# First block of a hybrid decoder layer: one input piece between the compression weight halves, two units in halves, scores inside a unit, the scan in parts

## The chip, the cores and the metric

The kernel runs on one core of one Trainium2 chip. The metric is the device time of one execution in microseconds. Three runs of the kernel before took 2506.0, 2507.16 and 2510.76 us; the median is 2507.16 us.

## The reference

A trunk of two equal layers over 256 tokens of width 1024, all in float32. The first block of each layer normalises x, multiplies it by one wide input projection and hands the columns to three branches: a native sparse attention (compressed, selected and windowed keys), a gated linear recurrence (RG-LRU) and a Mamba-2 mixer. The branches are gated, multiplied by branch weights and added to x. The second block (PEER) retrieves single-neuron experts by product keys. What the change touches is all in the first block:

```python
# 15 compressed blocks of 32 tokens, stride 16, for keys and for values
blk = t[:, cmp_idx] + pe[None, None, :, None, :]
return jax.nn.gelu(blk @ w1) @ w2
...
s_c = jnp.einsum('bqghd,bcgd->bghqc', qb, k_cmp) * SCALE      # compressed scores
s_s, s_w = q . k over selected and windowed keys, softmax each
...
b = mult * (i * xc)                                            # RG-LRU
_, h = lax.associative_scan(linear_recurrence_combine, (a, b), axis=1)
```

## The kernel before, in words

The weights come as a stream of *pieces* of 1 MB (128 x 2048 floats), 66 a layer, numbered u. SyncE issues `load(u)` (L315) in order of u into a ring of 4 slots; piece u waits until the work on piece u-4 has been multiplied (`s_proj`). Nearly every piece is split for the exact float32 product: ScalarE writes the rounded high part (`split_hi`, L350, into a ring of 3), VectorE the low part (`split_lo`, L358), and TensorE makes three passes, hi by hi, lo by hi and hi by lo (`three_passes`, L367 to L369). Such a product of one piece with all 256 tokens is a *unit*: 48 matmuls, in two halves of 24 (`feature_half`), one for each 128 output rows. ScalarE takes the result out of PSUM (`take`, L948) and mostly splits the piece three further on in the same step (`next_hi`, `filler`). Each engine runs its list in the order that the program writes; only semaphores join them.

Pieces 8 to 11 are the recurrence's input (LX to LX+3). Pieces 12 to 15 are the compression's first weight matrix, two for keys and two for values (`UNSPLIT`): they aren't split; 64 matmuls (L668) multiply them with shifted blocks that VectorE makes (L1370) from keys and values which TensorE turned (L631, `kv_turned`) and ScalarE took (L1005 to L1010). Pieces 16 to 21 (XBC to XBC+5) are the Mamba input, 22 on the gates.

TensorE's order around the compression is: LX+2, `kv_turned`, LX+3, four weight pieces in two halves of two (L668), two turns of q (L643), XBC, turn of the compressed hidden rows (L679), two turns of q, XBC+1, second compression product (L688, L692), XBC+2, turn (L698), XBC+3, compressed scores of the first tile of 128 tokens (L711), XBC+4. VectorE meanwhile rotates q by position (L1311 to L1321), makes the recurrence's convolution in two halves of four steps (L1378, L1380), takes the turned q (L1396), normalises the compressed keys (L1418 to L1429), and splits XBC to XBC+5 in between.

The attention then runs over 16 pairs n (two tiles of 8). Of each n: TensorE makes scores (L724), VectorE adds mask and takes the maximum (`row_max`, L1466, L1470), ScalarE the exponentials (L1042), VectorE `coefficients` (L1476, L1477), GpSimd scales (L1186), TensorE turns (L740), ScalarE and VectorE take (L1050, L1487), TensorE attends (L763, L767). Between these stands one unit of gates for each n (`FILL[n]`). At n = 8, where the tile changes, come the second compressed scores and two units, `BETWEEN[0]` and `BETWEEN[1]`, each followed by the scores of one pair. VectorE at that place also makes the second half of the recurrence: one product (L1512) and four scans (L1516), with the coefficients of pair 8 between the second and third scan, and it splits `FILL[9]` after them and after `row_max(9)`.

Of the kernel before, what the change touches and what calls it, by code (L numbers as in the profile page):

```python
# [66 lines left out]
UNSPLIT = range(2 * W1K, 2 * XBC0)  # L67
# [119 lines left out]
def trunk(nc, x_in, pos_tok, pos_row, const, wstream, small, rows, mix_row, ffn_row, subkeys, xstream, out):  # L187
    V, A, PE, PO = nc.vector, nc.scalar, nc.tensor, nc.gpsimd
    with ExitStack() as ctx:
# [93 lines left out]
        def layer_programs(layer):  # L283
# [17 lines left out]
            def nth(u):  # L301

                return u if u < UNSPLIT.start else u - len(UNSPLIT)

            def piece(n):

                return n if n < UNSPLIT.start else n + len(UNSPLIT)
# [98 lines left out]
            with mix:  # L406
# [54 lines left out]
                with mid:  # L461
# [65 lines left out]
                    def place(u):  # L527
                        if u < UNSPLIT.start:
                            return u
                        if u < XBC + 5:  # L530
                            return u - 4
# [50 lines left out]
                    def mixer_tensor(pe):  # L582
# [44 lines left out]

                        def kv_turned(t):
# [17 lines left out]
                        for u in range(FIRST, LX + 3):  # L646
# [7 lines left out]
                        for t in range(NT):  # L654
                            kv_turned(t)
                        unit(LX + 3)


                        for half in range(2):
                            w1 = []  # L660
                            for j in range(2):
                                u = UNSPLIT.start + 2 * half + j
# [3 lines left out]
                            for r in range(8):  # L666
                                for j in range(2):
# [132 lines left out]
                        for n in range(1, len(units) + 1):  # L800
# [115 lines left out]
                    def mixer_scalar(act):  # L916
# [37 lines left out]
                        def filler(u):  # L954

                            if u < LG:
                                dst = xbcT[:, 2 * (u - XBC):2 * (u - XBC) + 2, PAD:]
# [33 lines left out]
                        for n in range(3):  # L991
# [8 lines left out]
                        for t in range(NT):  # L1000
                            act.wait_ge(s_kvt, past(s_kvt) + t + 1)
                            for j, c in enumerate((0, 3)):
                                for g in range(G):
# [4 lines left out]
                                    else:  # L1008
# [8 lines left out]
                        act.wait_ge(s_proj, past(s_proj) + UNSPLIT.stop)  # L1017
# [3 lines left out]
                        filler(XBC)  # L1021
# [7 lines left out]
                        filler(XBC + 1)  # L1029
# [1415 lines left out]
```

## Time and profile before

| what | value |
|---|---|
| profiled execution, its own time | 2510.31 us |
| its span | 2508.4 us |
| TensorE matmul busy | 2450.2 us, 98% |
| VectorE, ScalarE, GpSimd busy | 69%, 55%, 32% |
| mean granted TensorE clock | 0.993 |
| chain of work that ended last, TensorE's share | 88% |

The span runs from the first to the last instruction on record; 1.9 us of the execution lie around it. Times in the rows are from the span's start. The first layer's first block takes roughly the first 400 us; the second layer's lies some 1247 us later. A granted clock of 1.00 is the full 2.4 GHz level, 0.50 the 1.2 GHz level.

### The profile page before, as it was taken

To read this page: it belongs to the slowest core of one execution; us is meant where nothing else is said; L and a number is where in the kernel's file an instruction comes from. 1 tells how busy PE (TensorE), PEld (TensorE's weight loads), DVE (VectorE), ACT (ScalarE), POOL (GpSimd) and SP (SyncE) were. 2 spreads that over 40 slices of the span, in tenths; PEclk is the share of its full clock that TensorE was granted. 3 is DMA by queue.
4 is the path that set the end of the run, shared out by engine and by line. 5 is a ranking of instruction groups with operands and counts; after the bars stand their busy time and mean duration, and the time that the engine had idled before them with its cause. 6 is when DMAs were issued, how large, how long until landed. Compare 5 with 4: busy or idle time off the path is not lost.

```text
span 2508.4 us, 45247 instructions
## 1 busy us (share of the span) xinstructions
PE 2450.2 (98%) x18518; PEld 2269.1 (90%) x18518; DVE 1729.8 (69%) x2726; ACT 1388.0 (55%) x2190; POOL 796.9 (32%) x436
## 2 busy tenths in 40 slices
PE   8999999999999999999999999999999999999999
PEld 8898899999999988888798989999999999888887
DVE  6878777499577755555678786764986778555555
ACT  5487564444566654445554965644445666544443
POOL 0011200188898830000000112002888988200000
PEclk9999999999999999999999999999999999999999
DMA  6533335355444455566555333453554444556655
GB/s 253 189 131 114 111 135 193 120 184 184 165 147 150 146 174 194 194 208 236 182 185 185 120 118 117 137 184 133 184 184 163 144 151 146 181 193 193 193 193 168
DMA packets 95963, 419.35 MB, mean 167 GB/s; under 512 B 10768, under 2 KB 11152, under 8 KB 78864
## 3 DMA queue, kind: packets, MB, share of 16 engines
q1 hardware_dynamic: 95760, 416.47, 48.6%
q8 instruction: 149, 2.44, 0.4%
q14 instruction: 54, 0.44, 0.0%
HBM read 415.38 MB, written 1.05 MB: 166 GB/s over the span
## 4 chain that ended last, share of the span: by engine, by line
PE 88%; DVE 6%; DMA 2%; ACT 2%; POOL 1%; issue 0%; SPq 0%; DVEq 0%; ACTq 0%
PE bank L2041 26%; PE bank L367 18%; PE bank L368 17%; PE bank L369 17%; PE bank L2022 3%; DMA xr<-in_xstream 1%; PE bank L763 1%; PE bank L740 1%; PE bank L724 1%; DVE ring_lo L358 1%; POOL xr_lo L1738 1%; DVE choice L2224 1%; PE bank L1880 1%; PE bank L780 1%; PE bank L859 1%; PE bank L872 1%
## 5 line engine op out<-in xcount | busy, mean ns | idle before, releaser
L1733 ACT ACTIVATE xr_hi<-xr 128x1024 fp32r<-128x1024 f32 x512 | 542.3, 1060 | 689.9 <-DMA xr<-in_xstream 686.1
L1738 POOL TENSOR_TENSOR xr_lo<-xr,xr_hi 128x1024 fp32r<-128x1024 f32 x256 | 619.8, 2425 | 409.7 <-ACT xr_hi L1733 408.6
L367 PE MATMUL bank<-featH,xr_hi 128*128 128x256 f32 x2048 | 586.6, 286 | 7.7 <-POOL xr_lo L1738 7.7
L368 PE MATMUL bank<-featL,xr_hi 128*128 128x256 f32 x2048 | 575.2, 281 | 0.0
L369 PE MATMUL bank<-featH,xr_lo 128*128 128x256 f32 x2048 | 574.8, 281 | 0.0
L1738 DVE TENSOR_TENSOR xr_lo<-xr,xr_hi 128x1024 fp32r<-128x1024 f32 x256 | 313.7, 1225 | 303.9 <-ACT xr_hi L1733 303.7
L367 PEld LDWEIGHTS bank<-featH,xr_hi 128*128 128x128 f32 x2048 | 386.0, 188 | 9.1 <-POOL xr_lo L1738 4.8
L368 PEld LDWEIGHTS bank<-featL,xr_hi 128*128 128x128 f32 x2048 | 386.4, 189 | 0.0
L369 PEld LDWEIGHTS bank<-featH,xr_lo 128*128 128x128 f32 x2048 | 385.8, 188 | 0.0
L367 PE MATMUL bank<-featH,ring_hi 128*128 128x256 f32 x1232 | 357.1, 290 | 14.9 <-DVE ring_lo L358 13.7
L368 PE MATMUL bank<-featL,ring_hi 128*128 128x256 f32 x1232 | 351.3, 285 | 0.0
L369 PE MATMUL bank<-featH,ring_lo 128*128 128x256 f32 x1232 | 350.8, 285 | 0.0
L1186 POOL TENSOR_TENSOR tok_z<-tok_z,rst 128x512 f32<-128x512 f32 (+1 forms) x32 | 51.6, 1611 | 864.1 <-DVE rst L1477 864.1
L2041 PE MATMUL bank<-xr_hi,p_hi 128*128 128x512 f32 x1024 | 316.4, 390 | 2.7 <-DVE acts_lo L2272 1.5
L2041 PE MATMUL bank<-xr_lo,p_hi 128*128 128x512 f32 x1024 | 315.3, 389 | 0.0
L2041 PE MATMUL bank<-xr_hi,acts_lo 128*128 128x512 f32 x1024 | 315.3, 389 | 0.0
L358 DVE TENSOR_TENSOR ring_lo<-ring,ring_hi 128x2048 fp32r<-128x2048 f32 x120 | 273.9, 2286 | 59.8 <-ACT ring_hi L350 58.1
L350 ACT ACTIVATE ring_hi<-ring 128x2048 fp32r<-128x2048 f32 x120 | 229.1, 1909 | 98.6 <-PE bank L369 76.5
L367 PEld LDWEIGHTS bank<-featH,ring_hi 128*128 128x128 f32 x1232 | 237.8, 193 | 23.2 <-issue 19.0
L368 PEld LDWEIGHTS bank<-featL,ring_hi 128*128 128x128 f32 x1232 | 237.8, 193 | 0.1
L369 PEld LDWEIGHTS bank<-featH,ring_lo 128*128 128x128 f32 x1232 | 237.6, 193 | 0.0
L2041 PEld LDWEIGHTS bank<-xr_hi,p_hi 128*128 128x128 f32 x1024 | 191.3, 188 | 45.7 <-DVE acts_lo L2272 3.9
(352 smaller groups left out, 4106.9 us busy)
## 6 DMA issues: line engine op xcount, KB each, us to landing
xr<-in_xstream SPq DMA_DIRECT2D x512, 512.0 KB, 3.3
ring<-in_wstream SPq DMA_DIRECT2D x128, 1024.0 KB, 4.9
smw<-in_small SPq DMA_DIRECT2D x4, 617.0 KB, 9.9
first<-in_wstream SPq DMA_DIRECT2D x4, 512.0 KB, 6.9
first<-in_wstream SPq DMA_DIRECT2D x2, 1024.0 KB, 8.3
subk<-in_subkeys SPq DMA_DIRECT2D x2, 1024.0 KB, 7.4
x<-in_x SPq DMA_DIRECT2D x2, 512.0 KB, 5.8
big<-in_mix_row SPq DMA_DIRECT2D x2, 512.0 KB, 4.8
```

What stands on the lines that cost most here:

```text
L350: A.activation(hi, w, ACT.Copy).then_inc(s_hi, 1)
L358: V.tensor_tensor(lo, w, hi.bitcast(F32), ALU.subtract).then_inc(s_lo, 1)
L367: PE.matmul(o, s_hi_lo[0], m_hi_lo[0], start=first, stop=False)
L368: PE.matmul(o, s_hi_lo[0], m_hi_lo[1], start=False, stop=False)
L369: return PE.matmul(o, s_hi_lo[1], m_hi_lo[0], start=False, stop=last)
L724: mm = PE.matmul(bank[2 + g][:, b * nk:(b + 1) * nk], qT[g * DH:(g + 1) * DH, i, t * P:(t + 1) * P], kT[g * DH:(g + 1) * DH, b, 0:nk], sta ...
L740: tr = PE.transpose(bank[4 + k][:, j * P:(j + 1) * P], sc[:, n % 2, j, k * P:(k + 1) * P], ident)
L1186: PO.tensor_tensor(sc[:, n % 2, :, 0:nk], sc[:, n % 2, :, 0:nk], over(rst[:, n % 2, 2, :], nk), ALU.mult).then_inc(s_scaled, 1)
L1733: A.activation(xr_hi[:, m % XR], xr[:, m % XR], ACT.Copy).then_inc(s_xhi, 1)
L1738: (PO if m < NKEY else V).tensor_tensor(xr_lo[:, m % XR], xr[:, m % XR], xr_hi[:, m % XR].bitcast(F32), ALU.subtract).then_inc(s_xlo_pool ...
L2022: mm = PE.matmul(bank[g % GBANKS][:, j * P:(j + 1) * P], hots(g)[:, j, 0, :], hots(g)[:, j, third, :], start=third == 1, stop=third == 3)
L2041: mm = PE.matmul(bank[2 * t + h][:], p, w[:, m % XR, h * 512:(h + 1) * 512], start=first_one and i == 0, stop=last and i == NKEY - 1)
```

## The change

The stream is laid out anew: XBC (now `FIRST_XBC`) becomes piece 14 and stands between the two weight halves, which are pieces 12, 13 and 15, 16. TensorE turns keys and values before LX+2 instead of after it; after LX+3 it multiplies the first weight half, then the unit of piece 14, then the second half. The unit of piece 18 (XBC+2) is cut into halves around two turns of q and the second compression product, that of piece 19 around the turn of the compressed keys. At the tile change the scores of pair 8 stand between the two halves of `BETWEEN[0]` instead of behind it. ScalarE and VectorE follow: VectorE splits piece 14 before the second rotation of q, and makes three of the four convolution steps of the second half only after the compressed keys are normalised. At n = 8 VectorE now splits `FILL[9]` right after `row_max(8)`, then makes the coefficients of pair 8 and `row_max(9)`, and only then the recurrence's product and its first two scans; the last two scans come at n = 9 behind `row_max(10)`, ahead of the split of `FILL[10]`.

```diff
-UNSPLIT = range(2 * W1K, 2 * XBC0)
+W1_HALVES = ((2 * W1K, 2 * W1K + 1), (2 * W1K + 3, 2 * W1K + 4))
+FIRST_XBC = 2 * W1K + 2
+UNSPLIT = W1_HALVES[0] + W1_HALVES[1]
...
+                        def half_unit(u, f):
+                            if f == 0:
+                                room(place(u))
+                            mm = feature_half(pe, u, f, feat, bank_of(place(u))[:, f * S:(f + 1) * S])
+                            if f:
+                                mm.then_inc(s_proj, 1)
...
-                        for u in range(FIRST, LX + 3):
+                        for u in range(FIRST, LX + 2):
                             unit(u)
...
                         for t in range(NT):
                             kv_turned(t)
+                        unit(LX + 2)
                         unit(LX + 3)
...
+                        hidden(0)
+                        unit(FIRST_XBC)
+                        hidden(1)
                         for n in range(2):
                             q_turned(n)
-                        unit(XBC)
+                        unit(XBC + 1)
...
+                        half_unit(XBC + 2, 0)
                         for n in range(2, 4):
                             q_turned(n)
-                        unit(XBC + 1)
...
-                        unit(XBC + 2)
+                        half_unit(XBC + 2, 1)
+                        half_unit(XBC + 3, 0)
                         pe.wait_ge(s_ckn, past(s_ckn) + 1)
...
-                        unit(XBC + 3)
+                        half_unit(XBC + 3, 1)
...
-                                unit(BETWEEN[0])
+                                feature_half(pe, u, 0, feat, bank_of(place(u))[:, 0:S])
                                 scores(n)
+                                feature_half(pe, u, 1, feat, bank_of(place(u))[:, S:2 * S]).then_inc(s_proj, 1)
                                 unit(BETWEEN[1])
                                 scores(n + 1)
...
-                        for n in range(3):
+                        for n in range(2):
                             take(LX + n, lxT[:, 2 * n:2 * n + 2, PAD:])
...
+                        take(LX + 2, lxT[:, 4:6, PAD:])
+                        split_hi(act, FIRST_XBC)
                         take(LX + 3, lxT[:, 6:8, PAD:])
-                        for n in range(HIS):
-                            split_hi(act, XBC + n)
+                        split_hi(act, XBC + 1)
+                        take(FIRST_XBC, xbcT[:, 0:2, PAD:])
...
+                        for n in range(2, 4):
+                            split_hi(act, XBC + n)
...
+                        split_lo(dve, FIRST_XBC)
                         q_rope(1)
...
                             lru_conv(k, 0)
-                            if k == 1:
-                                split_lo(dve, XBC)
-                        q_taken(0)
-                        q_taken(1)
+                            if k == 0:
+                                split_lo(dve, XBC + 1)
+                            elif k == 2:
+                                split_lo(dve, XBC + 2)
+                                q_taken(0)
+                                q_taken(1)
                         lru_conv(0, 1)
-                        lru_conv(1, 1)
-                        split_lo(dve, XBC + 1)
-                        q_taken(2)
-                        q_taken(3)
-                        lru_conv(2, 1)
-                        split_lo(dve, XBC + 2)
-                        lru_conv(3, 1)
+                        split_lo(dve, XBC + 3)
...
+                        q_taken(2)
+                        q_taken(3)
+                        for k in range(1, CONV):
+                            if k == 2:
+                                split_lo(dve, XBC + 4)
+                            lru_conv(k, 1)
...
                                 row_max(n)
-                                lru_scan(1, lambda: coefficients(NP))
+                                split_lo(dve, FILL[n + 1])
+                                coefficients(n)
...
                                 row_max(n + 1)
-                            if n + 1 in FILL:
+                            if n == NP:
+                                lru_gated(1)
+                                lru_scan(1, range(0, 2))
+                            elif n == NP + 1:
+                                lru_scan(1, range(2, HALF_LRU))
+                            if n + 1 in FILL and n != NP:
                                 split_lo(dve, FILL[n + 1])
```

## Rows read from the trace of the kernel before

**Rows 1.** The page: TensorE's busy time, share of the span, instructions.
```profile
PE 2450.2 (98%) x18518; PEld 2269.1 (90%) x18518; DVE 1729.8 (69%) x2726; ACT 1388.0 (55%) x2190; POOL 796.9 (32%) x436
```

**Rows 2.** The waits of TensorE's matmuls: us in total, times, longest.
```profile
PE bank L367 <- DVE ring_lo L358: 14.1, 10, 3.7
...
PE bank L668 <- DMA ring<-in_wstream: 1.6, 2, 0.8
...
PE bank L724 <- DVE tok_z L1466: 1.5, 2, 0.7
PE bank L740 <- POOL tok_z L1186: 1.4, 2, 0.7
...
PE bank L668 <- DVE big L1370: 1.1, 2, 0.5
```

**Rows 3.** Timeline of TensorE at XBC: start, length, instruction, [idle before].
```profile
96.21 0.55 PE L367 MATMUL bank<-featH,ring_hi 128*128 128x256 f32 x1 [3.74 <-DVE ring_lo L358]
...
104.75 0.31 PE L679 MATMUL bank<-cst,xbcC 31*128 31x31 f32 x4
```

**Rows 4.** Stretches: length, busy time by engine, granted clock, DMA share, GB/s.
```profile
96.00:102.00 6.00, 5.79 (x27) 5.82 (x28) 5.82 (x15) 4.93 (x5) 0.00 (x0) 0.50 0.58 243
153.30:159.10 5.80, 5.80 (x48) 5.64 (x48) 5.66 (x11) 5.80 (x9) 1.04 (x1) 1.00 0.34 144
231.00:235.00 4.00, 3.63 (x19) 3.66 (x20) 3.93 (x8) 1.28 (x5) 1.89 (x1) 0.62 0.00 0
```

**Rows 5.** Timeline of ScalarE: the high parts of pieces 16 and 17.
```profile
91.75 1.91 ACT L350 ACTIVATE ring_hi<-ring 128x2048 fp32r<-128x2048 f32 x1 [6.71 <-DMA ring<-in_wstream]
95.30 1.91 ACT L350 ACTIVATE ring_hi<-ring 128x2048 fp32r<-128x2048 f32 x1 [1.63 <-DMA ring<-in_wstream]
```

**Rows 6.** The load of piece 17 alone, issued at 87.37 us: its time to landing.
```profile
DMA to landing us min/median/max: 7.9/7.9/7.9
```

**Rows 7.** Chain that ended last, 82 to 107 us: VectorE's steps, start and length.
```profile
82.01 2.08 DVE big L1370 x4
84.09 0.17 DVE st L1311
...
89.27 1.24 DVE tok_q L1321
...
90.64 1.39 DVE xcT L1378 x4
...
93.77 2.29 DVE ring_lo L358
```

**Rows 8.** Timeline of VectorE: its idle time ahead of the first compressed maximum.
```profile
127.50 0.47 DVE L1440 SCALAR_TENSOR_TENSOR lxT<-bank,cst 128x120 f32<-128x120 f32 x2 [6.15 <-PE bank L711]
```

**Rows 9.** Timeline of VectorE at the tile change.
```profile
220.65 1.22 DVE L1512 TENSOR_TENSOR big<-big 128x1024 f32<-128x1024 f32 x1
221.90 1.27 DVE L1516 TENSOR_TENSOR_SCAN xcT<-big 128x256 f32<-128x256 f32 x2
...
223.36 2.92 DVE L1516 TENSOR_TENSOR_SCAN xcT<-big 128x256 f32<-128x256 f32 x2
226.49 1.29 DVE L1466 SCALAR_TENSOR_TENSOR tok_z<-bank,cst 128x512 f32<-128x512 f32 x2 [0.21 <-DVE xcT L1516]
...
228.95 2.28 DVE L358 TENSOR_TENSOR ring_lo<-ring,ring_hi 128x2048 fp32r<-128x2048 f32 x1
```

**Rows 10.** Timeline of GpSimd: the scalings of pairs 8 and 9.
```profile
223.52 2.21 POOL L1186 TENSOR_TENSOR tok_z<-tok_z,rst 128x1024 f32<-128x1024 f32 x1 [23.36 <-DVE rst L1477]
232.19 1.89 POOL L1186 TENSOR_TENSOR tok_z<-tok_z,rst 128x1024 f32<-128x1024 f32 x1 [6.46 <-DVE rst L1477]
```

**Rows 11.** Chain that ended last, 208 to 243 us: `FILL[9]`'s first matmul and what follows the unit.
```profile
231.37 0.36 PE bank L367
...
238.81 1.02 PE bank L763 x16
```

**Rows 12.** Timeline of ScalarE at n = 11: the take of the turned probabilities behind the silu.
```profile
263.65 0.58 ACT L1050 ACTIVATE lxT<-bank 128x512 f32<-128x512 f32 x1
```

More of the change, by code:

```diff
@@ L66 @@
 HALF_W = WCOL // 2
-UNSPLIT = range(2 * W1K, 2 * XBC0)
+W1_HALVES = ((2 * W1K, 2 * W1K + 1), (2 * W1K + 3, 2 * W1K + 4))
+FIRST_XBC = 2 * W1K + 2
+UNSPLIT = W1_HALVES[0] + W1_HALVES[1]
+SPLIT = tuple(u for u in range(PIECES) if u not in UNSPLIT)
 HALF_LRU = 4
@@ L301, in nth @@
             def nth(u):
-                return u if u < UNSPLIT.start else u - len(UNSPLIT)
+                return SPLIT.index(u)
             def piece(n):
-                return n if n < UNSPLIT.start else n + len(UNSPLIT)
+                return SPLIT[n] if n < len(SPLIT) else PIECES
             def load(sp, u):
@@ L527, in place @@
                     def place(u):
-                        if u < UNSPLIT.start:
+                        if u < UNSPLIT[0]:
                             return u
+                        if u == FIRST_XBC:
+                            return UNSPLIT[0]
                         if u < XBC + 5:
@@ L655, in mixer_tensor, with hidden @@
                             kv_turned(t)
+                        unit(LX + 2)
                         unit(LX + 3)
-                        for half in range(2):
+                        def hidden(half):
                             w1 = []
-                            for j in range(2):
-                                u = UNSPLIT.start + 2 * half + j
+                            for j, u in enumerate(W1_HALVES[half]):
                                 pe.wait_ge(s_blk, past(s_blk) + 2 * half + j + 1)
@@ L826, in mixer_tensor @@
                                 cmp_scores(1)
-                                unit(BETWEEN[0])
+                                u = BETWEEN[0]
+                                room(place(u))
+                                feature_half(pe, u, 0, feat, bank_of(place(u))[:, 0:S])
                                 scores(n)
+                                feature_half(pe, u, 1, feat, bank_of(place(u))[:, S:2 * S]).then_inc(s_proj, 1)
                                 unit(BETWEEN[1])
@@ L956, in filler @@
                             if u < LG:
-                                dst = xbcT[:, 2 * (u - XBC):2 * (u - XBC) + 2, PAD:]
+                                f = 0 if u == FIRST_XBC else 2 * (u - XBC)
+                                dst = xbcT[:, f:f + 2, PAD:]
                             elif u < MG:
@@ L1020, in mixer_scalar @@
                         ge.then_inc(s_chg, 1)
-                        filler(XBC)
+                        for n in range(2, 4):
+                            split_hi(act, XBC + n)
+                        filler(XBC + 1)
                         act.wait_ge(s_cht, past(s_cht) + 1)
@@ L1508, in lru_mult, with lru_gated, lru_scan @@
                             V.tensor_scalar(gate_r[:], gate_r[:], 1e-30, None, ALU.max).then_inc(s_lm, 1)
-                        def lru_scan(half, between=None):
+                        def lru_gated(half):
                             dve.wait_ge(s_lsq, past(s_lsq) + half + 1)
                             dch.link(V.tensor_tensor(gate_i[:], gate_i[:], gate_r[:], ALU.mult))
-                            for j in range(HALF_LRU):
-                                if between and j == HALF_LRU // 2:
-                                    between()
+                        def lru_scan(half, tiles):
+                            for j in tiles:
                                 dch.add(V.tensor_tensor_scan(xcT[:, HALF_LRU * half + j, :], lru_a[:, j, :], gate_i[:, j, :], 0.0,
@@ L1518, in lru_scan @@
                             dch.settle()
-                            dve.sem_inc(s_lruh, 1)
-                        split_lo(dve, XBC + 4)
+                            if tiles.stop == HALF_LRU:
+                                dve.sem_inc(s_lruh, 1)
                         dve.wait_ge(s_sig, past(s_sig) + 1)
@@ L1562, in mixer_vector @@
                                 elif n == at + 3 and half == 0:
-                                    lru_scan(half)
+                                    lru_gated(half)
+                                    lru_scan(half, range(0, HALF_LRU))
                                     ssm_conv(3, half)
```

5 lines of the change are left out of this document (2 added, 3 removed).

## The prediction

> **What bounds the kernel now.** Read the page's busy times first: TensorE's matmuls fill 98% of the span [rows 1], so a gain is either work taken from TensorE or one of its gaps. The change takes no matmul away; it can only close gaps. Second, the list of TensorE's waits: the largest on VectorE's low parts is 14.1 us in 10 waits, the longest 3.7, and with it come smaller ones on the compression's weights and shifted blocks and, in pairs, on the scores' buffers and GpSimd's scaling [rows 2]. Each of the last four is "2 times": once a layer. Third, the timeline at the longest wait. TensorE stands for 3.74 us ahead of XBC, and XBC's unit then runs from 96.21 to 104.75, 8.54 us [rows 3], although a unit at full clock takes 5.9: one filled 5.80 of 5.80 us with 48 matmuls at a granted clock of 1.00, where 96 to 102 us shows 0.50, the 1.2 GHz level [rows 4]. So a wait costs twice, once by itself and once in the clock behind it: here 3.74 + 2.64.
>
> The reason for the wait is the ring. XBC's high part starts at 91.75, as its load lands, after ScalarE idled 6.71 us; that of the next piece waits for its own load until 95.30 [rows 5]. VectorE then needs until 93.77 + 2.29 for XBC's low part [rows 7]. XBC's slot is free only when the first weight half is multiplied, so its load, its two parts and its unit lie behind each other with only the second half and two turns to cover them.
>
> The second place is the tile change. VectorE makes product and scans from 220.65 to 226.28, then `row_max(9)`, and the low part of `FILL[9]` only at 228.95 to 231.23 [rows 9]; TensorE starts that unit at 231.37 and ends it at 238.81, 7.44 us, with the granted clock at 0.62 over 231 to 235 [rows 4, 11]. The wait before it is 2.4 us (the layer's share of rows 2), after gaps of 0.74 (scores(10) on `row_max(9)`) and 0.70 (turn(8) on GpSimd) [rows 2].
>
> **Compression, today's price for a layer.** Wait for the shifted blocks 0.54, for weight pieces 0.80 (half of each pair) [rows 2], for XBC 3.74, slow clock 2.64 [rows 3]: 7.7 us.
>
> **What the new order leaves there.** Turning keys and values one unit earlier starts ScalarE's copies and VectorE's blocks about 5 us sooner. VectorE had idled until 82.01 for them [rows 7]; now it is free at 79.5 after the first rotation, makes the four blocks in 2.08 us by 81.6, and the first weight half starts with LX+3's end near 82.8: the 0.54 goes. The 0.80 goes too, since pieces 15 and 16 now have a whole unit to land in. Piece 14 can load when LX+2 is done, about 77.4 (the turns, 1.04 us of TensorE, are now ahead of it); an undisturbed load took 4.7 to 4.9, so it lands at 82.2, high part to 84.1, low part to 86.5. The first half ends at 86.5. The unit follows with nothing to wait for, or 0.1. This unit is what now covers the chain.
>
> Next is piece 17 (XBC+1). Its slot is freed by the first half, 86.5, as that of piece 16 is, and it is issued second: 7.9 us to land [rows 6], 94.8. High part 1.91, low part 2.29 [rows 5, 7] and some 0.3 of handshakes: TensorE may start at 99.3. If piece 17 lands 2.95 behind piece 16 (as the later of the four loads did), it is 98.8. TensorE is there at 86.6 + 5.9 (piece 14) + 3.6 (second half, 64 such matmuls are 7.3 us) + 1.1 (two turns) = 97.2. A wait of 1.6 to 2.1 stays; I take 1.9. VectorE is free in time: split to 86.5, rotation 6.5 (84.09 to 90.50 in rows 7) to 93.0, first convolution step 1.39 to 94.4. Bound below: 0; above: 3.7, today's wait.
>
> Behind it VectorE: two convolution steps of 1.7 to 102.5, low part of 18 to 104.8; TensorE asks for it at 105.3. Margin 0.5. Low part of 19 at 111.5, asked at 114; keys normalised 3.2 us after the second compression product (111.2), 114.5, asked at 117: this is what halving the units buys, a half unit of 2.95 us as cover for each answer. Without it a wait of up to 1 us would follow. The three convolution steps moved behind it, 4.9 us, and the low part of 20, 2.3, end at 123; TensorE's first compressed scores end about 121.5. Before, VectorE idled 6.15 us ahead of the compressed maximum [rows 8]; that idle pays for the moved steps, and the maximum is late by 1.5 with a unit of 5.9 to cover it. The 32 weight matmuls, the loads (one order, SyncE's wait for u-4 still) and the number of instructions stay. Cost of three more breaks in a unit: 0.1 each, between 0 and 0.3.
>
> Sum: 7.7 - 1.9 - 0.2 = 5.6 us a layer. If the low part of 18 slips behind its margin, or a load is slow, 0.3 goes: 5.3.
>
> **Tile change.** Price now: 0.74 + 0.70 + 2.41 + (7.44 - 5.9 = 1.54) = 5.4. New: scores(8) are made inside the first unit, 215.2 instead of 218.2 (old clock of the trace), so `row_max(8)`, right behind the compressed probabilities (216.5), ends at 219.1 and the low part of `FILL[9]` at 221.4, ten microseconds ahead of before. The 2.41 and the 1.54 go. `row_max(9)` starts with its scores at 225.1 instead of 226.49 [rows 9]: the 0.74 goes. Exponentials of pair 8 don't come sooner, because ScalarE first takes the unit that now ends 1.1 later and splits: 220.7 against 220.76. So turn(8) stays late.
>
> By how much depends on GpSimd. Its scaling of pair 8 took 2.21, that of pair 9 1.89, and the third scan, begun 0.16 before, took with the fourth 2.92 where two took 1.27 [rows 9, 10]. In the new order no scan lies beside a scaling: 0.3 sooner, 0.4 of the 0.70 is left. The Trainium skill, "SBUF — State Buffer", section "Who interferes with whom", says that a VectorE instruction with two SBUF inputs and a GpSimd instruction that reads SBUF exclude each other for a whole instruction; a scan has two. The trace agrees: 2.92 against 1.27. By it VectorE gains 1.6 us here; without it the scans would cost that again.
>
> What is late next: the last two scans, 1.3, stand before the low part of `FILL[10]`. `row_max(10)` ends near 233.8, scans 235.1, low part 237.4; TensorE asks for it at 237.4 (3.3 after the unit's end at 234.1). Wait 0 to 0.3, and 1.6 more if a scaling falls on them; I take 0.1. Then n = 11: silu and table loads hold ScalarE's take until 263.65 + 0.58 [rows 12]. The attend that needs it comes with the end of `FILL[12]`: 238.81 [rows 11] plus three rounds of 9.2 (unit 5.9, attend, turn and scores 3.3), 266.4, so there are 2.2 us of room. Silu follows VectorE's convolution and `row_max(12)`, which come only 0.5 sooner while TensorE comes 4.6 sooner, and the take comes 1.5 sooner: a wait of 0.9. Sum: 5.4 - 0.4 - 0.1 - 0.9 = 4.0, between 2.4 (the scans' collision) and 5.
>
> **Total.** (5.6 + 4.0) x 2 layers = 19.2, less 0.5 for scatter of the loads: 18.7. Behind these places TensorE releases all others, so the gain passes on. The profiled execution took 2510.3, 3.1 above the median; 2491.6 there, and 2488.5 against the median of 2507.16.
>
> **Rivals.** 1. *The clock falls again.* The trace dropped it after waits of 3.74 and 2.41 [rows 3, 4]; the left wait of 1.9 is near the second. A fall costs 1.5 to 2.6 a layer behind XBC+1. For it: closeness of 1.9 to 2.4; against: the 2.41 had 1.4 us of other gaps within the 4 us before it. Result: 18.7 - 3 to 5 = 14 to 16, 2491 to 2493. The Trainium skill, "TensorE: Matmul & The Clock Gate", section "HAM oscillation — how this bites in real kernels", describes just this, a wait for data followed by a burst at half clock; by it 2492. The trace agrees on its two places.
> 2. *Only the tile change pays.* Piece 17 lands as late relative to its use as 16 did, VectorE's longer list delays 18, and a fall of the clock follows: 3.7 + 2.6 left of 7.7. Gain 1.4 + 4 a layer, 10 to 11: 2496. For it: VectorE is busy nearly throughout [rows 7]. Against: a whole unit more stands before it.
> 3. *Given back later.* If the second tile is set by ScalarE and VectorE (gelu, silu, late scans), the 4.0 comes back as waits of attends, and the compression's gain goes the same way: within 5 us of before, 2503 to 2510. Against: before, the take at n = 11 had 2.2 us of room, others more.
> 4. *Slower.* VectorE becomes the bound from the low part of 18 on: its 6.15 of idle is used up, every split then waits in its list, and TensorE stands at each of six units until the tile's end. From a lateness of 5.6 us a layer on there is no gain, and with two falls of the clock (2.6 each) it is a loss: about 2512. It decides only if VectorE is over 6 us later than placed here.
>
> **Chances.** Forecast 0.60; rival 1 0.17; rival 2 0.11; rival 3 0.07; rival 4 0.05. What this measurement can't tell from no change is 0.2%, 5 us. Faster by more: 0.60 + 0.17 + 0.11 = 0.88; the same: 0.07; slower: 0.05. Range: low end from both places at their best (7.7 and 5.0 a layer, less 1 left each: 22 us, 2485, and 1 for scatter, 2484); high end takes in rivals 1 and 2 with their lower prices, 2500.
>
> **What would show it.** In the changed profile: no wait for the weight pieces or shifted blocks; one wait of 1.6 to 2.1 before the unit of piece 17, released by the low part; high part of piece 17 begun on its load's landing; the unit of `FILL[9]` 5.9 long with no wait; turn(8) waiting 0.3 to 0.4; a wait of about 0.9 of attend(11) on ScalarE; both scan pairs 1.3 long; both falls of the clock gone in each layer's first block but for chance. A wait over 1 us at piece 18, 19 or `FILL[10]`, or granted clock 0.5 behind piece 17, would make the steps wrong.

## The result and the profile after

| | before | changed |
|---|---|---|
| median of the runs | 2506.84 us (2506.00 to 2510.76) | 2485.07 us (2482.26 to 2485.36) |
| ratio, 95% interval | | 0.9908 (0.9890 to 0.9925) |
| profiled execution, its own time | 2510.31 us | 2484.94 us |
| its span | 2508.4 us | 2483.0 us |
| mean granted clock | 0.993 | 0.998 |

The changed kernel is 22 to 23 us faster; forecast were 18.7, to 2488.5 us. The direction, both places and the mechanism are as predicted. The size is not: the gain lies 3 to 4 us above the forecast, and the time at the low end of the range (0.9908 of the 2507.16 us that the forecast started from is 2484.1). Repeated on another chip the changed kernel took 2484.74 us, ratio 0.9905 (0.9890 to 0.9920).

The two traces differ by 25.4 us, more than the medians do, because the execution profiled of before lay 3.5 us above the median of its runs. Comparing the start of the same matmul in both traces, 10.8 us are gained by the end of the first layer's first block and 11.1 in the second layer's. Nearly all of the other 3.5 us lie in the expert stages, where GpSimd's low parts were waited for 7.7 us before and 4.8 after, and where the clock was down for a shorter time; these move from execution to execution, and the change touches nothing there. In a second trace of the changed kernel the first layer's expert stages gave 0.8 us where they gave 3.1 here, and over all traces of this case they lie between 1.8 us lost and 3.8 gained.

TensorE's waits after the change (total, times, longest), against [rows 2]. The waits for weight pieces, shifted blocks, `tok_z` by maximum and `tok_z` by GpSimd are gone from the list, which leaves out waits under 0.15 us, and VectorE's low parts fall from 14.1 us to 5.0:

```profile
PE bank L1882 <- DVE h_tok L1851: 6.7, 2, 3.4
PE bank L370 <- DVE ring_lo L361: 5.0, 8, 1.5
PE bank L370 <- POOL xr_lo L1772: 4.8, 6, 1.5
...
PE bank L780 <- ACT lxT L1074: 0.3, 2, 0.2
```

The page's busy times, against [rows 1]. No matmul was taken away; TensorE's busy time falls by 9 us, which is work no longer done at half clock:

```profile
PE 2441.2 (98%) x18518; PEld 2259.3 (91%) x18518; DVE 1723.8 (69%) x2726; ACT 1388.7 (56%) x2190; POOL 797.1 (32%) x436
```

**Compression.** TensorE's timeline: the unit of piece 14 follows the first weight half without a wait, the second half and the turns follow, and before the unit of piece 17 stands the one wait that is left. It takes the place of [rows 3]:

```profile
83.63 2.98 PE L680 MATMUL bank<-ring,big 128*31 128x256 f32 x26
86.59 0.36 PE L370 MATMUL bank<-featH,ring_hi 128*128 128x256 f32 x1
...
92.44 3.65 PE L680 MATMUL bank<-ring,big 128*31 128x256 f32 x32
96.02 1.09 PE L656 MATMUL bank<-cst,tok_q 128*128 128x128 f32 x8
98.66 0.36 PE L370 MATMUL bank<-featH,ring_hi 128*128 128x256 f32 x1 [1.54 <-DVE ring_lo L361]
...
104.50 0.31 PE L695 MATMUL bank<-cst,xbcC 31*128 31x31 f32 x4
```

The unit behind the wait is over after 5.8 us where it had taken 8.5, because the clock stays up. The stretches: length, busy time by engine, granted clock, DMA share, GB/s, against [rows 4]: that over the unit of piece 17, and the one where the tile changes:

```profile
98.60:104.60 6.00, 5.95 (x52) 5.84 (x52) 5.93 (x10) 3.90 (x3) 0.00 (x0) 1.00 0.69 287
...
231.00:235.00 4.00, 3.96 (x33) 4.00 (x34) 3.90 (x12) 3.97 (x4) 0.01 (x1) 1.00 0.08 31
```

The chain behind the wait: the two loads issued at 86.6 and 87.0 us and their times to landing, the second being piece 17 (against [rows 6]), ScalarE's high part on its landing (against [rows 5]), and VectorE's timeline, low part and what comes up to the compressed maximum (against [rows 7, 8]):

```profile
DMA to landing us min/median/max: 5.1/6.1/7.2
```
```profile
94.20 1.91 ACT L353 ACTIVATE ring_hi<-ring 128x2048 fp32r<-128x2048 f32 x1 [7.99 <-DMA ring<-in_wstream]
```
```profile
96.22 2.29 DVE L361 TENSOR_TENSOR ring_lo<-ring,ring_hi 128x2048 fp32r<-128x2048 f32 x1 [1.83 <-ACT ring_hi L353]
...
118.50 3.38 DVE L1405 SCALAR_TENSOR_TENSOR xcT<-lxT,smw,xcT 128x256 f32<-128x256 f32 x8
122.10 0.47 DVE L1466 SCALAR_TENSOR_TENSOR lxT<-bank,cst 128x120 f32<-128x120 f32 x2 [0.22 <-DVE xcT L1405]
```

VectorE's idle time ahead of the maximum is spent, 6.15 us to 0.22, on the three convolution steps moved behind the keys. The unit of XBC+4 starts at 121.0 us where it started at 127.3: the compression gave 6.3 us in this layer and 6.8 in the other, whose wait was 1.30. (At 80 us, ahead of the first weight half, the changed kernel was already 0.2 us behind, so the place itself gave 6.5.)

**Tile change.** VectorE's timeline (against [rows 9]), GpSimd's scalings (against [rows 10]) and TensorE's (against [rows 11]):

```profile
212.68 2.28 DVE L361 TENSOR_TENSOR ring_lo<-ring,ring_hi 128x2048 fp32r<-128x2048 f32 x1
...
218.82 1.29 DVE L1492 SCALAR_TENSOR_TENSOR tok_z<-bank,cst 128x512 f32<-128x512 f32 x2 [1.99 <-PE bank L741]
...
222.53 1.27 DVE L1543 TENSOR_TENSOR_SCAN xcT<-big 128x256 f32<-128x256 f32 x2
...
227.19 1.26 DVE L1543 TENSOR_TENSOR_SCAN xcT<-big 128x256 f32<-128x256 f32 x2
228.60 2.29 DVE L361 TENSOR_TENSOR ring_lo<-ring,ring_hi 128x2048 fp32r<-128x2048 f32 x1
```
```profile
216.92 1.89 POOL L1210 TENSOR_TENSOR tok_z<-tok_z,rst 128x1024 f32<-128x1024 f32 x1 [23.08 <-DVE rst L1503]
224.89 1.90 POOL L1210 TENSOR_TENSOR tok_z<-tok_z,rst 128x1024 f32<-128x1024 f32 x1 [6.08 <-DVE rst L1503]
```
```profile
221.23 0.39 PE L370 MATMUL bank<-featH,ring_hi 128*128 128x256 f32 x1
227.09 0.44 PE L780 MATMUL bank<-lxT,tok_kv 128*64 128x128 f32 x4
...
231.03 0.36 PE L370 MATMUL bank<-featH,ring_hi 128*128 128x256 f32 x1 [0.54 <-DVE ring_lo L361]
...
255.54 0.44 PE L780 MATMUL bank<-lxT,tok_kv 128*64 128x128 f32 x4 [0.18 <-ACT lxT L1074]
```

The low part of `FILL[9]` is made at 212.7, its unit starts at 221.2 with no wait and takes 5.9 us; `FILL[10]` waits 0.54 for the low part that now stands behind the last scans. This place gave 4.5 and 4.4 us.

### The profile page after: what moved, and what is told of

Read it like the earlier page. It is cut to its first block, busy times and chain, and to the rows that moved or that the text cites. A ratio compares the mean times of both kernels' runs of the same rounds, so it can differ in the third digit from the quotient of the medians.

```text
span 2483.0 us, 45249 instructions
## 1 busy us (share of the span) xinstructions
PE 2441.2 (98%) x18518; PEld 2259.3 (91%) x18518; DVE 1723.8 (69%) x2726; ACT 1388.7 (56%) x2190; POOL 797.1 (32%) x436
## 4 chain that ended last, share of the span: by engine, by line
PE 88%; DVE 6%; DMA 3%; ACT 2%; POOL 1%; issue 0%; SPq 0%; DVEq 0%; ACTq 0%
PE bank L2075 27%; PE bank L370 18%; PE bank L371 17%; PE bank L372 17%; PE bank L2056 3%; DMA xr<-in_xstream 1%; DMA ring<-in_wstream 1%; DVE ring_lo L361 1%; POOL xr_lo L1772 1%; PE bank L780 1%; PE bank L741 1%; PE bank L757 1%; DVE choice L2258 1%; PE bank L1914 1%; PE bank L797 1%; PE bank L879 1%
```

## The experiments

All were run beside the kernel before. Ratios are to it; a microsecond is 0.0004. "First blocks" is the gain at the same matmuls in the profiled execution, first layer then second. Theory A, the prediction's: the gain is the wait taken away plus the time not spent at half clock behind it. The theories against it are in each expectation.

**Each part alone.** The changed kernel with the tile change's old order, on TensorE and VectorE:

```diff
-                                u = BETWEEN[0]
...
-                                feature_half(pe, u, 0, feat, bank_of(place(u))[:, 0:S])
+                                unit(BETWEEN[0])
                                 scores(n)
-                                feature_half(pe, u, 1, feat, bank_of(place(u))[:, S:2 * S]).then_inc(s_proj, 1)
...
-                                split_lo(dve, FILL[n + 1])
-                                coefficients(n)
+                                lru_scan(1, lambda: coefficients(NP))
...
```

> The changed kernel with the tile change as it was before (scores behind whole units, scan and splits in the old order); the compression part alone. Theory (two separate places, each paid by its own waits): the first blocks are 6.3 to 6.8 us a layer shorter up to the first compressed scores, and the tile change costs its old 5.4 again; gain about 13 us, 2493 to 2494, with the 2.4 us wait and the slow clock at FILL[9] back in both layers. Rival (the parts help each other: VectorE's convolution moved later makes the tile change worse, or the gain was mostly a chance of the clock): gain under 10 or over 16 us.

And the kernel before with these same lines the other way round, which is the tile change alone:

> The kernel before with the tile change alone (scores of pair 8 inside BETWEEN[0], FILL[9] split early, scan in parts). Theory: 4.4 to 4.6 us a layer, gain about 9 us, 2498; together with the compression part alone 22 us. In the trace no wait at FILL[9], 0.5 at FILL[10], the 3.7 us wait and the slow clock at XBC as before. Rival (parts not additive): gain under 6 or over 12 us.

Measured: compression alone 2493.51 us, 0.9939 (0.9926 to 0.9953), some 15 us; tile change alone 2499.37 us, 0.9962 (0.9949 to 0.9976), some 9.5. Together they make 24.8 against 23 for both: additive within the intervals. The first blocks show it more closely: 5.8 and 6.7 with compression alone, 4.6 and 4.3 with the tile change alone, 21.4 together, where the changed kernel has 21.9. (In the first kernel's first layer the 1.2 GHz level around `FILL[9]` lasted longer than before and cost 0.9 of the compression's gain.) Each kernel keeps the waits of the other place. TensorE's waits with compression alone, then with the tile change alone:

```profile
PE bank L370 <- DVE ring_lo L361: 8.6, 8, 2.4
PE bank L741 <- DVE tok_z L1489: 1.5, 2, 0.7
PE bank L757 <- POOL tok_z L1207: 1.4, 2, 0.7
```
```profile
PE bank L367 <- DVE ring_lo L358: 11.8, 10, 3.9
PE bank L668 <- DMA ring<-in_wstream: 1.5, 2, 0.8
PE bank L668 <- DVE big L1373: 1.1, 2, 0.5
```

So both places pay, and rivals 2, 3 and 4 are out.

**The halved units.** XBC+2 and XBC+3 whole again, with the turns and the second compression product ahead of them:

```diff
-                        half_unit(XBC + 2, 0)
                         for n in range(2, 4):
                             q_turned(n)
...
-                        half_unit(XBC + 2, 1)
-                        half_unit(XBC + 3, 0)
+                        unit(XBC + 2)
...
-                        half_unit(XBC + 3, 1)
+                        unit(XBC + 3)
```

> The changed kernel with pieces 18 and 19 as whole units: the turns of q and the second compression product before unit 18, the turn of the compressed keys between 18 and 19. Theory (the halves cover ScalarE's take of the hidden rows): TensorE waits about 1.8 us a layer for that take (it is there near 106, the copies end near 107.8) and the low part of 18 has room; loss against the changed kernel 3 to 4 us, 2488 to 2489. Rival, the prediction's own words (up to 1 us): a loss of 2 us or less. Second rival (halving costs more in breaks than it covers): no loss or a gain.

Measured: 2492.82 us, 0.9934 (0.9921 to 0.9948), 6.5 us worse than the changed kernel by the ratios. TensorE's timeline, and the stretches behind the new wait (length, TensorE's busy time, granted clock, DMA share, GB/s):

```profile
98.40 0.36 PE L370 MATMUL bank<-featH,ring_hi 128*128 128x256 f32 x1 [1.50 <-DVE ring_lo L361]
...
107.56 0.62 PE L703 MATMUL bank<-smw,xbcC 128*15 128x64 f32 x8 [1.71 <-ACT xbcC L1050]
...
108.97 0.37 PE L370 MATMUL bank<-featH,ring_hi 128*128 128x256 f32 x1
...
116.35 0.23 PE L713 MATMUL bank<-cst,xbcC 15*128 15x15 f32 x1
```
```profile
109.00:112.40 3.40, 3.40 (x19) 0.53 0.00 0
112.40:116.40 4.00, 4.00 (x34) 0.97 0.00 0
```

The wait is on ScalarE's copies of the turned hidden rows, not on VectorE. It is 1.7 us, as expected, and behind it the clock goes to the 1.2 GHz level, which the expectation (a loss of 3 to 4 us) had left out. The 1.71 us are longer than every wait that went without a fall (1.54 at most), so this wait may have done it alone; whether the 1.50 us ahead of the unit before had a part isn't shown. The unit takes 7.4 us in place of 5.9. In the second layer the level was down over the second compression product too, twice as long. Its stretches, with all engines:

```profile
1348.40:1351.80 3.40, 3.40 (x20) 3.20 (x21) 3.37 (x5) 1.20 (x1) 0.00 (x0) 0.50 0.24 99
1351.80:1355.00 3.20, 3.20 (x17) 3.20 (x17) 2.76 (x10) 0.20 (x1) 0.00 (x0) 0.50 0.00 0
```

So the halves were worth 3.4 us in one layer and 5.1 in the other of this trace, the slowest of its five runs, where the prediction had put "up to 1 us". That they bring a gain only because they hold up that of the rest is argued, not run: they weren't tried in the kernel before. The Trainium skill, "TensorE: Matmul & The Clock Gate", section "HAM oscillation — how this bites in real kernels", describes work at half clock behind a wait for data, of about 3 to 5 us in its example. This trace agrees on the half clock; the wait here was 1.71 us.

**The chain behind the wait, made longer.** ScalarE makes the high part of piece 17 only after the gelu, which itself follows the second weight half:

```diff
-                        split_hi(act, XBC + 1)
                         take(FIRST_XBC, xbcT[:, 0:2, PAD:])
...
-                        for n in range(2, 4):
+                        for n in range(1, 4):
                             split_hi(act, XBC + n)
```

> The changed kernel with ScalarE making the high part of piece 17 only after the gelu of the hidden rows. The wait before unit 17 grows from 1.5 to about 5.2 us. Theory (a wait costs twice, once more in the clock behind it): the granted clock falls to 0.5 behind it in both layers and the unit takes 8 to 9 us; 3.7 + 2.6 to 3.4 us a layer, 13 us in all, 2498. Rival (only the wait counts, the clock's falls are chance): 7.4 us in all, 2492.5, with unit 17 still 5.9 us long.

Measured: 2495.06 us, 0.9951 (0.9938 to 0.9965), some 10 us worse; first blocks 6.5 and 5.9. The waits in front of the unit are 4.29 us in both layers, not the 5.2 expected, and so the time is 3 us under the 2498 of the theory. TensorE's timeline and two stretches:

```profile
101.42 0.36 PE L370 MATMUL bank<-featH,ring_hi 128*128 128x256 f32 x1 [4.29 <-DVE ring_lo L361]
...
108.78 0.31 PE L695 MATMUL bank<-cst,xbcC 31*128 31x31 f32 x4
```
```profile
101.80:105.20 3.40, 3.40 (x18) 3.40 (x18) 3.33 (x8) 1.17 (x1) 0.00 (x0) 0.50 0.28 113
105.20:108.80 3.60, 3.60 (x33) 3.46 (x32) 3.60 (x6) 0.00 (x0) 0.00 (x0) 1.00 0.00 0
```

The waits grew by 2.75 and 2.99 us, 5.7 together, and the time by 10. Nearly all of the other 4 are the clock: the unit took 7.4 us in the first layer and 8.0 in the second, in place of 5.8. Against the rival, a longer wait alone would have cost 5.7. That a wait of this length costs nearly twice was worked out from the trace of before; here it is measured by making one.

**Keys and values turned after LX+2, as before.** ScalarE's take of LX+2 goes back with them; the rest as changed:

```diff
+                        unit(LX + 2)
                         for t in range(NT):
                             kv_turned(t)
-                        unit(LX + 2)
                         unit(LX + 3)
...
-                        for n in range(2):
+                        for n in range(3):
                             take(LX + n, lxT[:, 2 * n:2 * n + 2, PAD:])
...
-                        take(LX + 2, lxT[:, 4:6, PAD:])
```

> The changed kernel with the turns of keys and values behind unit LX+2 again. Theory (this move only pays the 0.5 us wait for the shifted blocks): first weight half waits 0.3 to 0.6, piece 14's low part still comes in time, first block about 0.5 us a layer longer, 2486. Rival (it also sets when piece 14 is split, since its split stands behind the blocks in VectorE's list): unit 14 waits 1 us or more, and with the 1.5 us wait behind it the clock falls; 2490 or above.

Measured: 2485.45 us, 0.9912 (0.9898 to 0.9926), which can't be told from the changed kernel, though the runs scatter from 2482.1 to 2490.9. The wait for the shifted blocks is back, 0.57 us a layer, as the theory had it, and isn't made up: in the second layer, with the wait at piece 17 as long as in the changed kernel, the compression gave 6.1 us instead of 6.8. The unit of piece 14 didn't wait, which speaks against the rival. A difference of 1 us in all is too small for the runs. What the profiled execution (2490.87 us) shows is how near the edge this is. TensorE's timeline and the stretch behind, the two loads' times to landing and ScalarE's high part:

```profile
100.32 0.36 PE L370 MATMUL bank<-featH,ring_hi 128*128 128x256 f32 x1 [2.74 <-DVE ring_lo L361]
...
107.69 0.31 PE L695 MATMUL bank<-cst,xbcC 31*128 31x31 f32 x4
```
```profile
100.60:104.00 3.40, 3.40 (x18) 3.40 (x17) 3.33 (x8) 3.15 (x2) 0.00 (x0) 0.51 0.77 320
```
```profile
DMA to landing us min/median/max: 5.4/6.9/8.4
```
```profile
95.86 1.91 ACT L353 ACTIVATE ring_hi<-ring 128x2048 fp32r<-128x2048 f32 x1 [9.92 <-DMA ring<-in_wstream]
```

Piece 17 took 8.4 us to land, not 7.2. The wait became 2.74 us, the clock fell, and the compression's gain was 3.1 us in that layer in place of 6.3: 1.2 for the longer wait, 0.6 for the shifted blocks, 1.5 for the unit at half clock (7.37 us in place of 5.84). In the other layer the wait was 1.35 and no fall followed. This is what rival 1 describes, here set off by one slow load.

**The tile change taken apart.** First the scores of pair 8 behind the whole unit, as before:

```diff
-                                u = BETWEEN[0]
-                                room(place(u))
-                                feature_half(pe, u, 0, feat, bank_of(place(u))[:, 0:S])
+                                unit(BETWEEN[0])
                                 scores(n)
-                                feature_half(pe, u, 1, feat, bank_of(place(u))[:, S:2 * S]).then_inc(s_proj, 1)
```

> The changed kernel, but the scores of pair 8 stand behind the whole unit BETWEEN[0] again. Theory (these scores bring nothing: the exponentials of pair 8 wait for ScalarE's split behind that unit, not for the scores): exponentials start within 0.2 us of before, turn(8) waits 0.1 to 0.3, first block at most 0.3 us a layer longer, time as the changed kernel's, 2484 to 2486. Rival (the early scores are what lets FILL[9] be split in time): a wait at FILL[9] again, 1 us a layer or more, 2487 or above.

Then VectorE's order as before, with the scores left inside the unit:

```diff
...
                                 row_max(n)
-                                split_lo(dve, FILL[n + 1])
-                                coefficients(n)
+                                lru_scan(1, lambda: coefficients(NP))
...
-                            if n == NP:
-                                lru_gated(1)
-                                lru_scan(1, range(0, 2))
-                            elif n == NP + 1:
-                                lru_scan(1, range(2, HALF_LRU))
-                            if n + 1 in FILL and n != NP:
+                            if n + 1 in FILL:
                                 split_lo(dve, FILL[n + 1])
```

> The changed kernel with VectorE's tile change as before (product and four scans around the coefficients of pair 8, then the maximum of pair 9, then the split of FILL[9]); the scores of pair 8 stay inside the unit. Theory (the order of VectorE's list is the whole tile-change gain): wait of about 2 us at FILL[9], 0.7 at the scores of pair 10, the fourth scan 2.3 us long beside GpSimd's scaling, 3.3 us a layer lost by waits and 1.7 more where the clock falls; 2492 to 2495. Rival (the early scores give VectorE enough room): under 1 us a layer lost, 2487.

Then VectorE's new order with the scan in one piece, all four behind `row_max(9)`:

```diff
                                 lru_gated(1)
-                                lru_scan(1, range(0, 2))
-                            elif n == NP + 1:
-                                lru_scan(1, range(2, HALF_LRU))
+                                lru_scan(1, range(0, HALF_LRU))
```

> The changed kernel with all four scans of the second half at n = 8, behind the maximum of pair 9; the early split of FILL[9] stays. Theory (moving the split ahead and the scans behind the maximum is the gain; parting the scans is not): the list of VectorE up to the split of FILL[10] has the same length, that split ends at the same time, pair 10's maximum comes 1.4 us later with room for it; first block within 0.3 us a layer of the changed kernel. Rival (the parting matters): GpSimd's scaling of pair 9 or the exponentials of pair 10 come late, a turn or an attend waits 0.7 us or more a layer.

Measured: scores behind 2482.97 us, 0.9906 (0.9890 to 0.9921), first blocks 11.2 and 11.1, as good as the changed kernel; the turn of pair 8 waits 0.2 us. VectorE's order as before 2492.51 us, 0.9938 (0.9924 to 0.9951): nearly the whole of the tile change is lost, 0.3 and 0.1 us of it remain. The scan in one piece 2487.50 us, 0.9919 (0.9906 to 0.9933), first blocks 11.2 and 11.1: in the traces no difference, and by the runs none that can be told (2.8 us above the changed kernel run beside it, with intervals that overlap). In the second of these VectorE's timeline, GpSimd's and TensorE's show the old picture again:

```profile
216.16 2.92 DVE L1542 TENSOR_TENSOR_SCAN xcT<-big 128x256 f32<-128x256 f32 x2
219.30 1.29 DVE L1492 SCALAR_TENSOR_TENSOR tok_z<-bank,cst 128x512 f32<-128x512 f32 x2 [0.21 <-DVE xcT L1542]
...
221.76 2.28 DVE L361 TENSOR_TENSOR ring_lo<-ring,ring_hi 128x2048 fp32r<-128x2048 f32 x1
```
```profile
216.33 2.21 POOL L1210 TENSOR_TENSOR tok_z<-tok_z,rst 128x1024 f32<-128x1024 f32 x1 [23.06 <-DVE rst L1503]
```
```profile
224.19 0.49 PE L370 MATMUL bank<-featH,ring_hi 128*128 128x256 f32 x1 [2.41 <-DVE ring_lo L361]
```

So of three edits at this place one pays: the recurrence put behind the low part of `FILL[9]` and behind `row_max(9)`. These two weren't run apart; by the waits, the first takes away 2.41 us and the slow clock, the second 0.74. The scores inside the unit and the parting of the scan are worth nothing measurable.

**A version aimed at the waits that are left.** All four turns of q around the second weight half, so that TensorE comes later to piece 17; and the last scans behind the split of `FILL[10]`:

```diff
-                        hidden(1)
                         for n in range(2):
                             q_turned(n)
+                        hidden(1)
+                        for n in range(2, 4):
+                            q_turned(n)
                         unit(XBC + 1)
...
-                        for n in range(2, 4):
-                            q_turned(n)
...
+                                q_taken(0)
+                                q_taken(1)
                                 split_lo(dve, XBC + 1)
...
-                            elif n == NP + 1:
-                                lru_scan(1, range(2, HALF_LRU))
...
+                            if n == NP + 1:
+                                lru_scan(1, range(2, HALF_LRU))
                             if n != NP:
```

> The changed kernel with two more moves: all four turns of q around the second weight half, ahead of unit 17 (VectorE takes the first two before it splits piece 17), and the last two scans behind the split of FILL[10]. Theory (the 1.5 us wait before unit 17 is the load's and can be filled with 1.1 us of turns; the 0.54 wait at FILL[10] is the scans'): 1.0 + 0.5 us a layer less, about 3 us below the changed kernel, 2482; waits 0.5 at unit 17 and none at FILL[10]. Rival (the turns only move the wait: the copies of q delay the low part of 17, or ScalarE's take of FILL[9], which waits for the scans, comes late and the attend of pair 9 waits): no gain.

Measured: 2485.81 us, 0.9909 (0.9895 to 0.9922), first blocks 11.4 and 12.1. The changed kernel and this one were run once more, on one chip:

> The changed kernel itself, beside the next one on the same chip: 2483 to 2486 us, ratio 0.990 to 0.992.

> The kernel with four turns of q around the second weight half and the last scans behind the split of FILL[10], on the same chip as the changed kernel. Theory: its first blocks are 0.7 to 1.0 us a layer shorter in the trace, 1.5 to 2 us in all, so 2482 to 2484. Rival: no difference that the runs can show, within 1 us of the changed kernel.

Measured: changed kernel 2484.74 us, 0.9905 (0.9890 to 0.9920), first blocks 11.3 and 11.1; this version 2484.22 us, 0.9902 (0.9887 to 0.9917), 11.2 and 12.1. TensorE's timeline in the first of its two traces shows where the rest went:

```profile
98.20 0.36 PE L370 MATMUL bank<-featH,ring_hi 128*128 128x256 f32 x1 [0.52 <-DVE ring_lo L361]
108.06 0.62 PE L704 MATMUL bank<-smw,xbcC 128*15 128x64 f32 x8 [0.68 <-ACT xbcC L1052]
```

The wait at piece 17 fell by 1.0 us, but the two turns were also the cover of the second compression product, which now waits 0.68 in the first layer of this trace and 1.18 in that of the other, though not in the second layers. The wait of 0.54 at `FILL[10]` is gone, and the attend of pair 9 waits 0.54 on ScalarE in its place, as the rival had it: moving the scans brought nothing. By the traces 0 to 0.6 us is left over in the first layer and 1 in the second, less than the theory's 1.5 in both. The runs don't show it: no version here beats the changed kernel by what can be measured.

Not taken apart is the compression: piece 14 between the weight halves and VectorE's three moved convolution steps were never run one without the other.

## Why the prediction came out as it did

**Right: the mechanism.** No wait for weights or blocks; one wait before piece 17, released by the low part of a piece whose load lands as the high part starts; `FILL[9]` 5.9 us long without a wait; both clock falls of the first blocks gone; both scan pairs 1.3 us long; the gain passed on to the end. The part of the sum by place was 5.6 + 4.0 a layer, measured 6.3 + 4.5 (6.5 + 4.5 from 80 us on) and 6.8 + 4.4.

**Wrong: the size of terms, nearly all towards caution.** The step that failed is the sizing of what would still be waited for behind the change. The sum leaves 1.9 + 0.2 in the compression and 0.4 + 0.1 + 0.9 at the tile change, 3.5 us a layer; the trace has 2.35 and 2.1. That is 2.5 us for both layers; today's price was 0.2 a layer too low, and 0.5 was taken off for scatter. With the three put right, 18.7 becomes 22.1, against 21.9 in the first blocks of the trace. The terms, in the prediction's words:
- "Next is piece 17 ... 7.9 us to land ... I take 1.9." The load took 7.2 and 6.9 us, the wait was 1.54 and 1.30: 0.4 and 0.6 more gain. The only row for this was one load of before that began 0.4 us behind another; the same load of the second layer took 6.8, so the sum rested on one draw from a wide spread. The "2.95 behind piece 16" stands in no row: it was 3.5 in that layer before, and is 2.5 in both layers now.
- "Cost of three more breaks in a unit: 0.1 each", of which only 0.2 was taken off. The halves of the two units show no idle time between them and the work that parts them.
- "Compression, today's price ... 7.7 us." It was one layer doubled, and it left out what XBC+1 waited: 0.18 us in that layer, 0.57 in the other. Both are within the 14.1 us in 10 of [rows 2], of which I had used the longest alone. Both went. In the second layer the slow clock cost 2.3 us and not 2.64, so that the price of either layer was 7.9.
- "0.3 sooner, 0.4 of the 0.70 is left" at turn(8): 0.1 was. GpSimd's scaling took 0.3 less, as said; it also began 0.3 sooner, since the coefficients no longer stand behind the first two scans.
- "The take comes 1.5 sooner: a wait of 0.9" of attend(11), the largest error, 0.7 a layer: it came 8.7 sooner, 2.4 apart from the compression's 6.3, and the wait was 0.18. ScalarE had idled 1.2 us for TensorE's unit ahead of its own take there; this idle time I had not seen, and it went with TensorE's being early.
- "I take 0.1" at `FILL[10]`: 0.54, the one error the other way.
- "Less 0.5 for scatter of the loads" was taken off and never came.

Put right, the first layer's sum is 7.7 + 0.2 - 1.5 = 6.4 and 5.4 - 0.1 - 0.5 - 0.2 = 4.6, against 6.5 (from 80 us on) and 4.5 in the trace: the working holds with its terms as measured.

**The range.** Its low end stood for 22 us of gain and 1 for scatter, so that the measured gain lies on it with no room beyond. The 22 (21.4 by its own terms) took 1 us as left at each place of each layer, 2 a layer, where the trace shows 2.35 and 2.1: what was written as the best case was nearly the plain one. The price it started from lacked XBC+1's wait, and the errors above are nearly all alike in sign; the range allowed for the scatter of one load and not for that.

**Right in kind, wrong in weight: the halves.** "A wait of up to 1 us would follow." It was 1.7, on ScalarE, and then the clock. I had looked at VectorE's list for what is late there and not at ScalarE's, where the high part of the next piece stands ahead of the copies. The prediction's sum did not need this number, but a reader who took it would have dropped the halves as worth 2 us when they are worth 6.

**Rival 1: the price was right.** It put a fall behind piece 17 at 1.5 to 2.6 us a layer. Where one happened, the unit took 7.37 (turns of keys and values late), 7.36 and 8.01 us (late high part) in place of 5.84: 1.5 to 2.2. Of its condition, a wait of 1.9 us, no run has an example. Waits of 1.1 to 1.5 us let the clock stand in both traces of the changed kernel, 2.74 did not. The waits in the section of the Trainium skill that it cites are longer (see the halved units), so "by it 2492" took over the description and not the size.

**SBUF.** Scans clear of GpSimd's scaling take 1.27 and 1.26 us a pair, beside it 2.92; the scaling 1.89, beside a scan 2.21. The Trainium skill, "SBUF — State Buffer", section "Who interferes with whom", says that a VectorE instruction with two SBUF inputs contends with a GpSimd instruction that reads SBUF, and these rows agree. But the gain here isn't the scan's 1.6 us: with the old order VectorE has the low part at 224.0, with the new at 215.0, and 1.6 is the smaller part of the 9.

## What to carry to other kernels

Price a wait of TensorE as it stands, and once more for the half clock where the granted clock of the trace falls behind waits of its length (here 1.71 us and more, not 1.54 and less); ask of each wait that is left how far it is from the next fall. A filler put between a transfer and its user pays even where it doesn't cover everything: here 10.5 us of work stood against 12.1 of load, both splits and handshakes, and 1.5 was left. When a filler is moved, look up whose cover it was. Work out each repeated stage from its own rows, not one and its double.

## What the runs showed that was not expected

- The length of the single wait parts the cases of this kernel. Over the thirteen traces, from 60 us on, the 1.2 GHz level came at every wait of TensorE of 1.71 us or more (1.71 and 1.72 with whole units; 2.41; 2.74; 3.2 to 4.3) and at no wait of 1.54 or less. It began up to 2 us before the wait's end or up to 1.7 after it. Nothing here was measured between 1.54 and 1.71, and the two shortest that brought a fall each had another wait (1.50, 1.37) 7.4 us of work before them, so that a single wait of 1.7 is untested.
- The second of two 1 MB loads issued 0.4 us apart took 6.9, 7.2 and 8.4 us to land where piece 17 was the second, the first of the two 5.1 or less in the changed kernel; at one issue pattern the spread is larger than most waits argued about here.
